# Prompt attention: which engine multiplies the probabilities by the reciprocal of their row's sum

## The chip, the cores and the metric

The kernel runs on one core of one Trainium2 chip. The metric is the device time of one execution in microseconds. The core has five instruction queues that run side by side and meet only at semaphores: TensorE (PE, with its weight loads PEld), VectorE (DVE), ScalarE (ACT), GpSimd (POOL) and SyncE (SP), which issues DMAs.

## The reference

The program is one step of a two-layer encoder: latent attention, a gated MLP mixer, and a squared-ReLU MLP behind each. The change lies in the attention of the 1024 prompt tokens, 8 heads:

```python
s = jnp.einsum('bqhd,bkhd->bhqk', qn, kn) + jnp.einsum('bqhr,bkr->bhqk', qr, kr)
s = s.astype(jnp.float32) * scale
visible = (k_pos[None, :] // CHUNK) <= (q_pos[:, None] // CHUNK)
s = jnp.where(visible[None, None], s, jnp.finfo(jnp.float32).min)
pr = jax.nn.softmax(s, axis=-1).astype(ckv.dtype)
```

The softmax is computed as exp(s - max) and then a multiplication by 1 / sum of the row. The probabilities then multiply the values.

## The kernel before

All matrix products are made in three passes: each float32 operand is held as a high part and a low part, and `mm3` multiplies hi by hi, hi by lo and lo by hi. ScalarE makes a high part by copying with rounding, VectorE makes the low part by subtracting the high part from the original.

`prompt_attention_phase` takes the heads two at a time, in four pairs. Each pair has a first stage, which projects queries, keys and values for 8 tiles of 128 tokens, and a second stage of 16 units, which is what the change touches. Unit n is 128 queries of one head: units 0 to 7 belong to the first head, 8 to 15 to the second. Because of the causal mask its width is 256, 256, 512, 512, 768, 768, 1024, 1024 keys, and the same again for the second head. Two units (2g, 2g+1) make a group of 256 queries, and the product with the values is made for a group at once.

One unit passes through these steps:

- `scores(n)`, TensorE: the scores into PSUM, in one bank up to 512 keys and two beyond. It waits for the exponentials of unit n-2, whose banks it takes.
- `maxes(n)`, VectorE: the row maximum (L949) and its negative times the scale (L950).
- `exps(n)`, ScalarE: exp of PSUM into `pr` in SBUF (L843), which also sums each row; a short second instruction of the same line reads the sum out to `total`.
- `normalise(n)`, VectorE: the reciprocal of `total` into `inv` (L955), then `pr` times `inv` in place (L956), which gives `pr_ready`.
- `probsT(n)`, TensorE: transposes of `pr` in 128 x 128 tiles into PSUM bank 4 or 5 (L1082), in one chunk of up to four tiles, or two chunks for more than 512 keys. A chunk waits until the chunk two before it has been read by both other engines (`pT_ready`).
- `probsT(n)`, ScalarE and VectorE: the high part of each chunk (L852), then its low part (L965).
- `values(g)`, TensorE: the three-pass product with the values, once both units of the group are transposed and split; ScalarE copies the result out (L859).

The order on each queue is fixed by the program, and every wait is for a semaphore's count. In turn n the queues hold:

- TensorE: scores of n+2, in turns 0, 6 and 14 one step of an unrelated modulation product (`mod1_step`, L157), transposes of n, and in even turns from 2 on the values of group n/2 - 1. Behind the last turn come the projection of the next pair's first tile (not in the last pair) and the values of group 7.
- VectorE: maximum of n+1, normalise n, low part of n-1; in turns 1, 9 and 14 small additions for the modulation, and in turns 13 and 14 the low part of the next pair's weights (L1202, not in the last pair).
- ScalarE: exponentials of n, high part of n-1, in even turns from 4 on a result copy; in turns 13 and 14 the high part of the next pair's weights (L1197, not in the last pair).

`mx`, `neg`, `total` and `inv` have two columns and `pr` two rows, used by turns for even and odd units.

Of the kernel before, what the change touches and what calls it, by code (L numbers as in the profile page):

```python
# [19 lines left out]
ALU = mybir.AluOpType  # L20
ACT = mybir.ActivationFunctionType
AX = mybir.AxisListType

P = 128
# [561 lines left out]
def prompt_attention_phase(nc, psum, io, ident, c_silu, cqT, ckvT, krT, ahead):  # L586
    PAIRS = H // 2
    QT = QL // P
    T = SEQ // P
    GR = T // 2  # L590
    N = 2 * 2 * GR
# [7 lines left out]
    def key_tiles(n):  # L599
        return 2 * unit(n)[1] + 2  # L600
# [11 lines left out]
    with Phase(nc, "patt") as ph:  # L612
# [41 lines left out]
        s_ready = ph.sem("s_ready")  # L654
        max_ready = ph.sem("max_ready")
        exp_ready = ph.sem("exp_ready")
        pr_ready = ph.sem("pr_ready")
        pT_raw = ph.sem("pT_raw")
        pT_hi_ready = ph.sem("pT_hi_ready")
        pT_ready = ph.sem("pT_ready")  # L660
# [21 lines left out]
        with nc.Block() as block:  # L682
# [111 lines left out]
            @block.scalar  # L794
            def _(act):
                def tile(p, t):
                    b, s = 2 * (t % 3), t % 2
                    act.wait_ge(proj_ready, p * T + (1 + t + 1))
                    act.wait_ge(r_ready, p * T + (t + 1))
                    act.wait_ge(ss_ready, p * T + (t + 1))  # L800
                    q, kv = psum[:, b, :], psum[:, b + 1, :]
                    HW = DN + DR
                    act.activation(v_hi[:, t, :], kv[:, 2 * DN:], ACT.Copy)
                    for n, (src, c) in enumerate((
                            (q[:, 0:DN], 0), (q[:, HW:HW + DN], HW), (q[:, DN:HW], DN), (q[:, HW + DN:2 * HW], HW + DN),
                            (kv[:, 0:DN], QW), (kv[:, DN:2 * DN], QW + DN))):
                        last = act.activation(junk[:, c:c + src.shape[1]], src, ACT.Square, accum_out=ss[:, s, n:n + 1])
                    last.then_inc(ss_ready, 1)

                def keys(p, t):  # L810
                    b, s = 2 * (t % 3), t % 2
                    act.wait_ge(r_ready, p * T + (2 + t + 1))
                    act.wait_ge(tokT_raw, p * T + (t + 1))
                    for j in range(2):
                        last = act.activation(k_tok[:, s, j, :], psum[:, b + 1, j * DN:(j + 1) * DN], ACT.Copy,
                                              scale=rs[:, s, 4 + j:5 + j])
                    last.then_inc(ktok_ready, 1)

                def tileT(p, t):
                    b, toks = 6, slice(t * P, (t + 1) * P)  # L820
                    act.wait_ge(tokT_raw, p * T + (2 + t + 1))
                    act.activation(qT_hi[:, :, toks], psum[:, b, :].rearrange("p (k n) -> p k n", k=4), ACT.Copy)
                    act.activation(kT_hi[:, :, toks], psum[:, b + 1, 0:2 * P].rearrange("p (k n) -> p k n", k=2),
                                   ACT.Copy).then_inc(tokT_hi_ready, 1)

                def guest(p):
                    q, k, HW = psum[:, 0, :], psum[:, 1, :], DN + DR
                    act.wait_ge(guest_raw, p + 1)
                    act.activation(guest_q, q[:, 0:QW], ACT.Copy)
                    for n, (src, c) in enumerate((  # L830
                            (q[:, 0:DN], 0), (q[:, HW:HW + DN], HW), (q[:, DN:HW], DN), (q[:, HW + DN:2 * HW], HW + DN),
                            (k[:, 0:DN], QW), (k[:, DN:2 * DN], QW + DN))):
                        last = act.activation(junk[:, c:c + src.shape[1]], src, ACT.Square,
                                              accum_out=ahead.ss_s[:, p, n:n + 1])
                    last.then_inc(guest_ready, 1)

                def exps(p, n):
                    s, width = n % 2, key_tiles(n) * P
                    if n == 5:
                        act.wait_ge(guest_stored, 16 * (p + 1))  # L840
                    act.wait_ge(max_ready, p * N + (n + 1))
                    act.wait_ge(pT_raw, p * C + (1 + before[max(n - 1, 0)]))
                    act.activation(pr[:, s, 0:width], flat(score_bank(n), width), ACT.Exp, bias=neg[:, s:s + 1], scale=SCALE,  # L843
                                   accum_out=total[:, s:s + 1]).then_inc(exp_ready, 1)

                def probsT(p, n):
                    g, i = n // 2, n % 2
                    for c, (k0, k1) in enumerate(chunks[n]):
                        m = before[n] + c
                        act.wait_ge(pT_raw, p * C + (1 + m + 1))  # L850
                        act.wait_ge(pv_ready, p * GN + (g + 1))
                        act.activation(pT_hi[g % 2][:, k0:k1, i * P:(i + 1) * P],  # L852
                                       psum[:, 4 + m % 2, 0:(k1 - k0) * P].rearrange("p (k n) -> p k n", n=P),
                                       ACT.Copy).then_inc(pT_hi_ready, 1)

                def out(p, g):
                    act.wait_ge(pv_ready, p * GN + (2 + g + 1))
                    act.wait_ge(stored[g % 2], p * (16 * GN // 2) + 16 * (g // 2 + 1))
                    act.activation(o[:, g % 2, :], psum[:, 6 + g % 2, 0:2 * P], ACT.Copy).then_inc(o_ready, 1)  # L859

                def w_split(p, i):
                    act.wait_ge(raw_in, p * 32)
                    act.wait_ge(proj_ready, p * T + 1)
                    ahead.split_hi(act, i)

                def pair(p, last):
                    for t in range(T + 1):
                        if t < T:
                            tile(p, t)
                        if t >= 1:  # L870
                            keys(p, t - 1)
                        if t >= 2:
                            tileT(p, t - 2)
                    guest(p)
                    exps(p, 0)
                    exps(p, 1)
                    tileT(p, T - 1)
                    for n in range(1, N + 1):
                        if 1 < n < N:
                            exps(p, n)  # L880
                        probsT(p, n - 1)
                        if n >= 4 and n % 2 == 0:
                            out(p, n // 2 - 2)
                        if n in SPLIT and not last:
                            w_split(p + 1, SPLIT.index(n))
                    out(p, GN - 1)

                act.sem_inc(ss_ready, 1)
                act.sem_inc(exp_ready, 2)
                act.sem_inc(o_ready, 2)  # L890
                for p in range(PAIRS):
                    pair(p, p == PAIRS - 1)

            @block.vector
            def _(dve):
# [53 lines left out]
                    step.run(dve.reduce_max(mx[:, s:s + 1], flat(score_bank(n), width), AX.X))  # L949
                    dve.tensor_scalar(neg[:, s:s + 1], mx[:, s:s + 1], -SCALE, None, ALU.mult).then_inc(max_ready, 1)  # L950

                def normalise(p, n, step):
                    s, width = n % 2, key_tiles(n) * P
                    dve.wait_ge(exp_ready, p * N + (2 + n + 1))
                    step.run(dve.reciprocal(inv[:, s:s + 1], total[:, s:s + 1]))  # L955
                    dve.tensor_scalar(pr[:, s, 0:width], pr[:, s, 0:width], inv[:, s:s + 1], None, ALU.mult  # L956
                                      ).then_inc(pr_ready, 1)

                def probsT(p, n):
                    g, i = n // 2, n % 2  # L960
# [7 lines left out]

                def pair(p, last):
                    step = Steps(dve, dve_step)  # L970
                    step.base = p * (2 * T + 2 * N + 6 + 4)
                    for t in range(T + 1):
                        if t >= 2:
                            tileT(p, t - 2, step)
# [3 lines left out]
                            finish_mod1(p, 0, step)  # L978
                    maxes(p, 0, step)
                    maxes(p, 1, step)  # L980
                    normalise(p, 0, step)
                    tileT(p, T - 1, step)
                    for n in range(1, N + 1):
                        if n + 1 < N:
                            maxes(p, n + 1, step)
                        if n < N:
                            normalise(p, n, step)
                        if n == 14:
                            read_mod1(p, 3)
                        probsT(p, n - 1)  # L990
                        if n in (1, 9):
                            read_mod1(p, 1 + n // 9)
                            finish_mod1(p, 1 + n // 9, step)
                        if n in SPLIT and not last:
                            ahead.split_lo(dve, p + 1, SPLIT.index(n))
                    finish_mod1(p, 3, step)
                    assert step.n == 2 * T + 2 * N + 6 + 4

                dve.sem_inc(mod_ready, 1)
                dve.sem_inc(mod1_ready, 1)  # L1000
# [10 lines left out]
            def _(pe):  # L1011
# [62 lines left out]
                    mm.then_inc(s_ready, 1)  # L1074

                def probsT(p, n):
                    pe.wait_ge(pr_ready, p * N + (n + 1))
                    for c, (k0, k1) in enumerate(chunks[n]):
                        m = before[n] + c
                        pe.wait_ge(pT_ready, p * C + (m + 1))  # L1080
# [2724 lines left out]
```

## Time and profile before

| | us |
|---|---|
| median of 3 runs | 2758.52 |
| lowest and highest | 2758.33, 2760.22 |
| the profiled execution's own time | 2763.28 |
| its span, first to last instruction | 2761.4 |

The profile gives for each group of instructions its line, engine, operation, output and inputs, shapes and count, then busy time and the mean length of one in ns. "Idle before" is the time for which the engine stood still before them, with what it waited for. In a timeline the columns are start, length, engine, line, operation and tiles, and in brackets the idle time before and its releaser. Instructions of one engine overlap a little at their ends, and a row with x2 merges neighbours. A matmul's end is modelled; its start is recorded. The second pair's 16 units lie between 280 and 339 us of the span, and the stages of the four pairs repeat each other closely.

### The profile page before, as it was taken

The page shows a single profiled execution, that of the slowest core. Times are in us where ns is not written, and L with a number is a line of the kernel's source. Part 1 is how long each engine was busy: PE and PEld are TensorE (multiplying, and loading weights), DVE is VectorE, ACT ScalarE, POOL GpSimd, SP SyncE. Part 2 cuts the span into 40 slices and gives each one's busy share as a digit, 9 for nine tenths or more (in the row PEclk, how much of TensorE's full clock was granted, in tenths as well). Part 3 has the DMA queues.
Part 4 walks back from the last instruction along what each step waited for, and adds up shares of the span by engine and source line. Part 5 has one row for each costly group of instructions (what it writes and reads, how often), then busy time and mean ns, then how long its engine had stood idle before and what let it go on. Part 6 is the DMA issues. An engine that isn't in the chain of part 4 may idle for free.

```text
span 2761.4 us, 45430 instructions
## 1 busy us (share of the span) xinstructions
PE 2649.2 (96%) x16628; PEld 2355.7 (85%) x16628; DVE 1878.2 (68%) x2672; ACT 1145.3 (41%) x2330; POOL 804.3 (29%) x736
## 2 busy tenths in 40 slices
PE   7989999899999999999999998999989999999998
PEld 4978888789997899999788887888879999988886
DVE  4677787655565876666898976224596666788886
ACT  3365556445552432222454444223342222354452
POOL 1122012055661222221144543000132222134444
PEclk9999999999999999999999999999999999999999
DMA  6244334322243333344534357124534333634446
GB/s 239 84 148 163 133 137 145 114 86 69 68 171 107 123 120 136 137 141 152 196 128 153 130 186 206 31 65 138 172 102 147 134 134 134 223 123 154 135 141 130
DMA packets 238061, 375.11 MB, mean 136 GB/s; under 512 B 18932, under 2 KB 182932, under 8 KB 234584
## 3 DMA queue, kind: packets, MB, share of 16 engines
q1 hardware_dynamic: 234408, 360.23, 39.0%
q0 software_dynamic: 3504, 12.91, 2.3%
q8 instruction: 92, 1.51, 0.2%
q14 instruction: 57, 0.47, 0.1%
HBM read 276.60 MB, written 96.48 MB: 135 GB/s over the span
## 4 chain that ended last, share of the span: by engine, by line
PE 54%; issue 6%; DVE 4%; DMA 2%; POOL 1%; ACT 1%; SPq 0%; POOLq 0%; DVEq 0%; ACTq 0%
PE psum L110 18%; PE psum L112 18%; PE psum L111 18%; DMA scratch_x_mid<-half_acc 1%; DVE half_h_lo L3052 1%; PE psum L3599 1%; DVE half_acc L3239 0%; POOL half_small L2899 0%; DMA half_m<-scratch_mixT 0%; DMA gate_x<-scratch_x_mid 0%; ACT half_tmp L2712 0%; PE psum L3610 0%; PE psum L3570 0%; DVE half_h_raw L3071 0%; SPq L134 0%
## 5 line engine op out<-in xcount | busy, mean ns | idle before, releaser
L2935 POOL TENSOR_TENSOR half_acc<-half_acc,half_tmp 128x512 f32<-128x512 f32 x174 | 292.2, 1693 | 356.0 <-ACT half_tmp L2712 268.8
L2712 ACT ACTIVATE half_tmp<-psum 128x512 f32<-128x512 f32 x174 | 104.0, 598 | 300.8 <-PE psum L112 300.6
L3239 DVE TENSOR_TENSOR half_acc<-half_acc,psum 128x512 f32<-128x512 f32 x240 | 160.5, 679 | 72.1 <-PE psum L112 53.3
L2605 ACT ACTIVATE half_snap_u<-psum 128x288 f32<-128x288 f32 x128 | 52.6, 411 | 285.8 <-PE psum L112 285.8
L110 PE MATMUL psum<-half_h_hi,half_w0q_hi 128*128 128x288 f32 x512 | 152.2, 297 | 7.2 <-DVE half_h_lo L3052 6.0
L110 PE MATMUL psum<-half_h_hi,half_w1q_hi 128*128 128x288 f32 x512 | 151.7, 296 | 1.6 <-DVE half_w1q_lo L3078 1.6
L111 PE MATMUL psum<-half_h_lo,half_w1q_hi 128*128 128x288 f32 x512 | 151.0, 295 | 0.0
L111 PE MATMUL psum<-half_h_lo,half_w0q_hi 128*128 128x288 f32 x512 | 151.0, 295 | 0.0
L112 PE MATMUL psum<-half_h_hi,half_w1q_lo 128*128 128x288 f32 x512 | 150.6, 294 | 0.0
L112 PE MATMUL psum<-half_h_hi,half_w0q_lo 128*128 128x288 f32 x512 | 150.5, 294 | 0.0
L3097 DVE TENSOR_TENSOR half_piece<-psum,half_snap_u 128x576 f32<-128x576 f32 (+1 forms) x68 | 49.1, 722 | 106.4 <-PE psum L112 79.0
L110 PE MATMUL psum<-half_w_hi,half_m_hi 128*128 128x512 f32 x288 | 117.0, 406 | 3.4 <-DVE half_w_lo L3010 1.8
L110 PE MATMUL psum<-half_h_hi,half_w0r_hi 128*128 128x288 f32 x384 | 115.1, 300 | 5.0 <-DVE half_h_lo L3052 5.0
L110 PE MATMUL psum<-gate_w_hi,gate_hT_hi 128*128 128x512 f32 x288 | 114.9, 399 | 2.0 <-issue 1.2
L112 PE MATMUL psum<-half_w_hi,half_m_lo 128*128 128x512 f32 x288 | 114.3, 397 | 0.0
L111 PE MATMUL psum<-half_w_lo,half_m_hi 128*128 128x512 f32 x288 | 114.1, 396 | 0.0
L111 PE MATMUL psum<-half_h_lo,half_w0r_hi 128*128 128x288 f32 x384 | 113.9, 297 | 0.0
L110 PE MATMUL psum<-half_h_hi,half_w1r_hi 128*128 128x288 f32 x384 | 113.7, 296 | 0.0
L112 PE MATMUL psum<-half_h_hi,half_w0r_lo 128*128 128x288 f32 x384 | 113.5, 296 | 0.0
L111 PE MATMUL psum<-half_h_lo,half_w1r_hi 128*128 128x288 f32 x384 | 113.3, 295 | 0.0
L112 PE MATMUL psum<-half_h_hi,half_w1r_lo 128*128 128x288 f32 x384 | 112.9, 294 | 0.0
L112 PE MATMUL psum<-gate_w_hi,gate_hT_lo 128*128 128x512 f32 x288 | 112.7, 391 | 0.0
(742 smaller groups left out, 8950.6 us busy)
## 6 DMA issues: line engine op xcount, KB each, us to landing
scratch_hid<-half_piece SPq DMA_DIRECT2D x64, 576.0 KB, 4.2
patt_mod_w<-in_ada_w_ffn SPq DMA_DIRECT2D x32, 768.0 KB
half_w0q_raw<-in_w SPq DMA_DIRECT2D x24, 1024.0 KB, 5.0
half_w1q_raw<-in_w SPq DMA_DIRECT2D x24, 1024.0 KB, 5.0
scratch_hid_sums<-half_sum SPq DMA_DIRECT2D x96, 256.0 KB, 2.8
patt_mod_w<-in_ada_w_att SPq DMA_DIRECT2D x16, 1024.0 KB, 5.0
half_s0q_raw<-scratch_hid SPq DMA_DIRECT2D x22, 512.0 KB
half_s1q_raw<-scratch_hid SPq DMA_DIRECT2D x22, 512.0 KB, 4.0
```

The lines of the kernel that those rows point to most:

```text
L110: pe.matmul(out, a_hi, b_hi, start=first, stop=False, skip_group_check=go_on)
L111: pe.matmul(out, a_hi, b_lo, start=False, stop=False, skip_group_check=go_on)
L112: return pe.matmul(out, a_lo, b_hi, start=False, stop=last, skip_group_check=go_on)
L2605: act.activation(out[:, grp, :], psum[:, bank(product, grp), 0:GN], ACT.Copy).then_inc(a.c.snap, 1)
L2712: act.activation(out, psum[:, o_bank_of(product, j), :], ACT.Copy).then_inc(a.c.taken, 1)
L2935: pool.tensor_tensor(part, part, snapshot(a, n, m), ALU.add).then_inc(a.c.added, 1 if i % SLABS else 3)
L3052: dve.tensor_tensor(a.h_lo[grp][slot][:], a.h_raw[grp][slot][:], f(a.h_hi[grp][slot][:]), ALU.subtract).then_inc(a.lo_ready[grp], 1)
L3097: dve.tensor_tensor(a.piece[i.par][f_][:, cols, side, :], psum[:, b:b + len(grps), 0:GN], snap[:, cols, :], ALU.add).then_inc(a.c.hid_read, 1)
L3239: dve.tensor_tensor(part, part, of, ALU.add).then_inc(a.c.read, 1)
L3599: mm = pe.matmul(psum[:, 6 + i // 4, (i % 4) * P:(i % 4 + 1) * P], g.ws[:, int(t == SAMPLE), i, :], g.z[:, t % 2, D + i * P:D + (i + 1) * ...
```

## The change

The multiplication by the reciprocal moves from VectorE to ScalarE, as a Copy activation whose scale is the column `inv`, in place on `pr`. VectorE keeps the reciprocal alone (`invert`), gives a new semaphore `inv_ready`, and ScalarE waits for it. `pr_ready` is given by ScalarE and starts two higher; VectorE now waits before a reciprocal until the multiplication two units before has read that column of `inv`. On ScalarE the new instruction stands behind the exponentials of the same unit and ahead of the high part of the unit before. The order on VectorE and TensorE stays.

```diff
@@ scalar queue
+                def normalise(p, n):
+                    s, width = n % 2, key_tiles(n) * P
+                    act.wait_ge(inv_ready, p * N + (n + 1))
+                    act.activation(pr[:, s, 0:width], pr[:, s, 0:width], ACT.Copy, scale=inv[:, s:s + 1]
+                                   ).then_inc(pr_ready, 1)
+
@@
                     guest(p)
                     exps(p, 0)
                     exps(p, 1)
+                    normalise(p, 0)
                     tileT(p, T - 1)
                     for n in range(1, N + 1):
                         if 1 < n < N:
                             exps(p, n)
+                        if n < N:
+                            normalise(p, n)
                         probsT(p, n - 1)
@@
+                act.sem_inc(pr_ready, 2)
@@ vector queue
-                def normalise(p, n, step):
-                    s, width = n % 2, key_tiles(n) * P
+                def invert(p, n):
+                    s = n % 2
                     dve.wait_ge(exp_ready, p * N + (2 + n + 1))
-                    step.run(dve.reciprocal(inv[:, s:s + 1], total[:, s:s + 1]))
-                    dve.tensor_scalar(pr[:, s, 0:width], pr[:, s, 0:width], inv[:, s:s + 1], None, ALU.mult
-                                      ).then_inc(pr_ready, 1)
+                    dve.wait_ge(pr_ready, p * N + (2 + n - 1))
+                    dve.reciprocal(inv[:, s:s + 1], total[:, s:s + 1]).then_inc(inv_ready, 1)
@@
                         if n + 1 < N:
                             maxes(p, n + 1, step)
                         if n < N:
-                            normalise(p, n, step)
+                            invert(p, n)
@@ tensor queue
                 def probsT(p, n):
-                    pe.wait_ge(pr_ready, p * N + (n + 1))
+                    pe.wait_ge(pr_ready, p * N + (2 + n + 1))
```

## Rows read from the trace of the kernel before

**Rows 1.** The page's first part: busy time, share of the span, instructions.
```profile
PE 2649.2 (96%) x16628; PEld 2355.7 (85%) x16628; DVE 1878.2 (68%) x2672; ACT 1145.3 (41%) x2330; POOL 804.3 (29%) x736
```

**Rows 2.** Busy time by stretch: the second pair's units; then VectorE on `pr` alone.
```profile
core 0: us, PE busy (x) PEld busy (x) DVE busy (x) ACT busy (x) POOL busy (x), PEclk, DMA share, GB/s
280.00:339.00 59.00, 57.44 (x571) 49.33 (x564) 43.73 (x105) 30.11 (x68) 1.14 (x2) 1.00 0.36 126
...
280.00:339.00 59.00, 8.86 (x16) 1.00 0.36 126
```

**Rows 3.** What TensorE waited for, 184 to 532 us: total, times, longest.
```profile
PE psum L1082 <- DVE patt_pT_lo L965: 5.3, 8, 1.1
PE psum L110 <- DVE patt_pT_lo L965: 1.6, 1, 1.6
```

**Rows 4.** ScalarE by line and shape, 184 to 532 us: busy, mean ns.
```profile
L852 ACT ACTIVATE patt_pT_hi<-psum 128x512 fp32r<-128x512 f32 x64 | 36.6, 597 | 62.8 <-PE psum L1082 62.8
L843 ACT ACTIVATE patt_pr<-psum,patt_neg 128x1024 f32<-128x1024 f32 x16 | 18.0, 1125 | 0.7
L843 ACT ACTIVATE patt_pr<-psum,patt_neg 128x768 f32<-128x768 f32 x16 | 14.5, 905 | 1.1
L843 ACT ACTIVATION_READ_ACCUMULATOR patt_pr<-psum,patt_neg 128x1 f32 x64 | 12.8, 200 | 0.0
L859 ACT ACTIVATE patt_o<-psum 128x256 f32<-128x256 f32 x32 | 12.3, 385 | 18.4 <-PE psum L112 18.4
L843 ACT ACTIVATE patt_pr<-psum,patt_neg 128x512 f32<-128x512 f32 x16 | 11.0, 690 | 7.5 <-DVE patt_neg L950 7.4
L843 ACT ACTIVATE patt_pr<-psum,patt_neg 128x256 f32<-128x256 f32 x16 | 7.7, 480 | 0.9 <-DVE patt_neg L950 0.9
```

**Rows 5.** ScalarE by line and shape, the whole program.
```profile
L1197 ACT ACTIVATE patt_wq_hi<-patt_q_raw 128x1152 fp32r<-128x1152 f32 x4 | 4.7, 1176 | 0.0
L1197 ACT ACTIVATE patt_wkv_hi<-patt_kv_raw 128x1024 fp32r<-128x1024 f32 x4 | 4.3, 1075 | 0.0
L1574 ACT ACTIVATE satt_o<-psum,satt_inv 128x256 f32<-128x256 f32 x8 | 3.8, 475 | 16.2 <-PE psum L1827 16.2
L843 ACT ACT_TABLE_LOAD x1 | 1.3, 1283 | 0.0
```

**Rows 6.** VectorE by line and shape, 184 to 532 us.
```profile
L965 DVE TENSOR_TENSOR patt_pT_lo<-psum,patt_pT_hi 128x512 fp32r<-128x512 f32 x64 | 42.4, 683 | 4.8 <-ACT patt_pT_hi L852 4.8
L949 DVE TENSOR_REDUCE patt_mx<-psum 128x1 f32<-128x1024 f32 x16 | 19.6, 1225 | 10.9 <-PE psum L1073 10.9
```

**Rows 7.** Timeline of three engines in turn 6 of the second pair (TensorE, ScalarE, VectorE rows).
```profile
299.25 0.82 PE L1082 MATMUL psum<-ident,patt_pr 128*128 128x128 f32 x6
...
299.45 1.23 DVE L949 TENSOR_REDUCE patt_mx<-psum 128x1 f32<-128x1024 f32 x1 [1.44 <-PE psum L1073]
...
300.78 0.15 DVE L955 RECIPROCAL patt_inv<-patt_total 128x1 f32<-128x1 f32 x1
...
299.89 0.87 ACT L852 ACTIVATE patt_pT_hi<-psum 128x512 fp32r<-128x512 f32 x2 [2.29 <-PE psum L1082]
...
302.47 1.06 PE L1082 MATMUL psum<-ident,patt_pr 128*128 128x128 f32 x8 [0.23 <-DVE patt_pT_lo L965]
```

**Rows 8.** Timeline of turns 13 to 15 of the second pair (VectorE, then TensorE rows).
```profile
324.24 1.35 DVE L1202 TENSOR_TENSOR patt_wq_lo<-patt_q_raw,patt_wq_hi 128x1152 fp32r<-128x1152 f32 x1
325.76 1.23 DVE L949 TENSOR_REDUCE patt_mx<-psum 128x1 f32<-128x1024 f32 x1 [0.17 <-PE psum L1073]
...
327.10 0.15 DVE L955 RECIPROCAL patt_inv<-patt_total 128x1 f32<-128x1 f32 x1
327.28 0.75 DVE L956 TENSOR_SCALAR patt_pr<-patt_pr,patt_inv 128x1024 f32<-128x1024 f32 x1
...
328.12 1.01 DVE L965 TENSOR_TENSOR patt_pT_lo<-psum,patt_pT_hi 128x512 fp32r<-128x512 f32 x2
...
328.94 1.06 PE L1082 MATMUL psum<-ident,patt_pr 128*128 128x128 f32 x8 [1.10 <-DVE patt_pT_lo L965]
331.99 0.38 PE L1082 MATMUL psum<-ident,patt_pr 128*128 128x128 f32 x2
```

**Rows 9.** Busy time by stretch around one fall of the clock, in a later stage.
```profile
1665.00:1667.50 2.50, 0.47 (x2) 0.42 (x3) 2.50 (x4) 2.15 (x4) 0.67 (x1) 1.00 0.46 187
1667.50:1670.90 3.40, 3.40 (x10) 2.65 (x9) 0.53 (x1) 1.79 (x4) 2.40 (x5) 0.50 0.85 122
```

More of the change, by code:

```diff
@@ L656, in prompt_attention_phase @@
         exp_ready = ph.sem("exp_ready")
-        pr_ready = ph.sem("pr_ready")
+        inv_ready, pr_ready = ph.sem("inv_ready"), ph.sem("pr_ready")
         pT_raw = ph.sem("pT_raw")
@@ L970, in pair @@
                     step = Steps(dve, dve_step)
-                    step.base = p * (2 * T + 2 * N + 6 + 4)
+                    step.base = p * (2 * T + N + 6 + 4)
                     for t in range(T + 1):
@@ L980, in pair @@
                     maxes(p, 1, step)
-                    normalise(p, 0, step)
+                    invert(p, 0)
                     tileT(p, T - 1, step)
@@ L996, in pair @@
                     finish_mod1(p, 3, step)
-                    assert step.n == 2 * T + 2 * N + 6 + 4
+                    assert step.n == 2 * T + N + 6 + 4
                 dve.sem_inc(mod_ready, 1)
```

## The prediction

> **What bounds the kernel now.** I read the page's busy times first: TensorE is busy for 96% of the span, ScalarE for 41% [rows 1]. An average says little about one stage, so I took the second pair's 16 units alone: of 59.0 us TensorE is busy for 57.4, VectorE for 43.7, ScalarE for 30.1 [rows 2]. The stage is TensorE's, and a microsecond counts only where TensorE stands still for it. Third, its waits: over all four pairs its matmuls wait 5.3 us in 8 places for the low part of the transposed probabilities before a transpose, and 1.6 us once before a value product [rows 3]. The multiplication itself is not what they wait for: in turn 14 it ends at 328.03, and the transposes start at 328.94, behind the first half of L965 [rows 8]. ScalarE has room by the average, but what matters is where: it stands idle for 62.8 us before the high parts of 512 columns, for TensorE's transposes [rows 4]. The change puts its instruction exactly ahead of those. Two timelines of the second pair show how near the chain runs to TensorE there [rows 7, 8].
>
> **What goes from VectorE.** Sixteen multiplications per pair, 8.86 us [rows 2], 35 us in all. VectorE is not the bound, so this is worth only what it shortens of TensorE's waits.
>
> **What comes to ScalarE.** Sixteen Copy activations per pair, SBUF to SBUF, with a per-partition scale. No row of before is exactly that. The exponentials have the same widths, the same float32 and one per-partition operand: 0.48, 0.69, 0.905 and 1.125 us for 256, 512, 768 and 1024 [rows 4]. A copy from SBUF without such an operand takes 1.075 for 1024 [rows 5], one from PSUM 0.385 for 256 and 0.597 for 512 [rows 4]. A copy of 256 with a per-partition scale takes 0.475 [rows 5], as long as the exponential of 256, so I take the exponentials' lengths: 4 x (0.48 + 0.69 + 0.905 + 1.125) = 12.8 us per pair, 51 in all. The lower bound is the plain copies' (0.385, 0.60, 0.84 by interpolation, 1.075), and, far from it, the length that VectorE needed. The upper bound is an exponential with its readout of 0.20 [rows 4].
>
> The 0.475 beside 0.385 says that a per-partition operand costs 0.09 us. The Trainium skill ("ScalarE: Activation LUTs", What ACT_TABLE_LOAD costs) states the same, about 93 ns for each such operand and 280 ns + 0.833 ns per column with one; by it 1024 columns would take an estimated 1.133 us, and the sum below would change by under 1 us. It speaks for the exponentials' row over the plain copies'.
>
> **What moves: the order.** The new waits matter more than the lengths. The multiplication of n waits for `inv` of n. On VectorE that reciprocal stands behind the maximum of n+1, which waits for the scores of n+1 on TensorE. Queued behind the waiting instruction on ScalarE are the high part of n-1 and the exponentials of n+1. For the high part wait the low part, the transposes that need its bank and the value product; for the exponentials waits the product of scores two units on. Before, the high part ran while VectorE still made the maximum: in turn 6 it starts at 299.89, the reciprocal comes only at 300.78 [rows 7]. Now it starts behind reciprocal and multiplication. VectorE's new wait, for the multiplication two units back, costs nothing: ScalarE ran it one turn earlier, ahead of the exponentials whose sum the same reciprocal needs.
>
> **The sum.** I laid the rows' lengths end to end in program order for one pair, each instruction starting when its engine is free and its semaphores have come. Neighbours overlap by 0.08 to 0.1, a hop between engines takes 0.03 to 0.05, and 0.12 from the low part to TensorE. Laid so for the kernel before, the last value product of the second pair starts at 335.6, the trace has 335.8, and the waits come where the trace has them (0.46 and 1.36 against 0.23 and 1.10 in the two places below). With the change:
>
> - Transposes of unit 6. The scores of 7 are there at 299.4. Then maximum, negation, reciprocal 1.23 + 0.15 + 0.15 with gaps of 0.1, 1.6; multiplication 1.125; high part 0.60; low part 0.68; hops 0.2 less overlap 0.1: 4.1. TensorE has work of its own for about 2.6 (from 299.25 to 302.47, less what it waited and the end of the scores) [rows 7]. It waits 1.45 in place of 0.46: +1.0.
> - Transposes of unit 14. From the reciprocal's end on, before: 0.75, 0.25 less overlap, and the first half of the low part, 1.66 to 328.94 [rows 8]. Now 1.125 + 0.60 + 0.68 with hops, 2.50: +0.84. The maximum of 15 also starts later. Before, VectorE had split the weights (1.35) by 325.6, just ahead of the scores at 325.7 [rows 8]. Now ScalarE's half of the split (1.18 [rows 5]) stands behind the multiplication of 13 (0.905) and the high part of 12, so VectorE's half ends 1.05 behind the scores. Together +1.9, a wait of 3.2 in place of 1.36.
> - Transposes of unit 15. From the start of 14's transposes: 0.40 + 0.60 for them and the first high part, then on ScalarE 0.385, 0.385, the second weight split 1.075, exponentials 1.125 + 0.20, reciprocal 0.15, multiplication 1.125, high part 0.60, low part 0.68, less overlaps: 4.6. TensorE has 2.9 to 3.05 of work until then [rows 8]. +1.6, where it hardly waited.
> - Twelve small places where the same chain comes 0.1 to 0.6 too late: scores of 4 by 0.41 (the exponentials of 2 now follow a multiplication and a high part), transposes of 8 by 0.58, value product 0 by 0.35, the second chunks of 4 and 12 by 0.29 each, and seven of 0.10 to 0.22. Together +3.1.
>
> That is 1.0 + 1.9 + 1.6 + 3.1 = 7.6 us per pair. The last pair has no weight splits: unit 14 costs 0.8, unit 15 0.65, the others as before, and its final value product waits 0.2 less: 5.5. Sum: 3 x 7.6 + 5.5 = 28.3. Nothing behind the stage hides it: the next pair's first ScalarE work waits for the last value product, and the next phase starts at a barrier. The profiled time goes from 2763.3 to 2791.6; it lies 4.8 above the median, so the median goes from 2758.5 to 2786.8, about 2787.
>
> With the multiplication at zero length the same layout gives only +1.3, with VectorE's lengths (0.355 to 0.755) +17.0, with the plain copies' +24.4, with the readout on top +39. So the length of the new instruction inside the chain is nearly all of it.
>
> **The rivals.**
>
> Shorter instruction: ScalarE runs it as fast as VectorE did. +17.0, 2775.5. Against it stands every SBUF row of ScalarE [rows 5].
>
> Hidden after all: the idle time of ScalarE before the high parts (62.8 us [rows 4], 2.29 of it in turn 6 [rows 7]) takes the multiplication in, and VectorE's relief comes off TensorE's waits: 0.75 in each of the four places at unit 14, 0.23 at each unit 6, 0.75 at the last value product [rows 3, 7, 8]. That is -4.7, 2753.8, not slower. It decides by whether the reciprocal is ready before the transposes of n-1 are. In turn 6 it is 0.9 late [rows 7].
>
> The clock: TensorE works at its upper level (1.00, 2.4 GHz) all through the stage. In a later stage it did 0.47 us of work in 2.5 us, and the clock then stood at 0.50 (1.2 GHz) for 3.4 us [rows 9]. A 3.2 us wait at unit 14 is longer than any before in these stages. A fall of 3.4 us costs 1.7 us of work, but it would fall on the value product ahead of unit 15's 1.6 us wait, which takes it in. A longer fall would cost up to 1.7 us in each pair: +28 to +35; with a somewhat longer instruction up to +39, 2797.5.
>
> Table loads: if Copy with a scale and Exp needed different tables, 128 loads of 1.28 us [rows 5] would come in, +164. One load serves the stage now, copies included, so this is remote.
>
> **How the numbers follow.** Forecast 2787 (+28, within +24 to +32): 0.60. Longer or with the clock, up to 2798: 0.20. Shorter, about 2775.5: 0.12. Hidden: 0.07, of which 0.02 for a gain over 0.2%. Table loads 0.01. The range 2775.5 to 2798 takes in both bounds of the length and the clock. A measurement can tell about 0.2%, 5.5 us, from no change: faster 0.02, within 0.06, slower 0.92.
>
> **What would show it.** ScalarE should have 64 new rows in place of L956 with means near 0.48, 0.69, 0.905 and 1.125. VectorE's idle time before L965 should grow from 4.8 us [rows 6] to some 80 us, since it now waits for the high part each turn. TensorE should stand still before the transposes of unit 14 for about 3.2 us in three pairs and 2.2 in the last, and for 1.6 before unit 15. The first stage of each pair should be as long as before. The prediction is wrong at its core if the high part still starts right behind the transposes, if the new means lie under 0.4 of a microsecond for 256, or if the pairs' unit stages grow by less than 4 us each.

## The result and the profile after

| | before | after |
|---|---|---|
| median of 3 runs, us | 2758.52 | 2786.66 |
| lowest and highest | 2758.33, 2760.22 | 2785.05, 2790.81 |
| the profiled execution's own time | 2763.28 | 2790.81 |
| its span | 2761.4 | 2789.1 |

The ratio is 1.0104, with a 95% interval of 1.009 to 1.0119. That is +28.1 us, between +25 and +33: slower, and by about what was forecast (+28.3).

First the new instruction. ScalarE by line and shape in the kernel after, 184 to 562 us (count, busy us, mean ns, idle time before with its releaser):

```profile
L858 ACT ACTIVATE patt_pT_hi<-psum 128x512 fp32r<-128x512 f32 x64 | 35.8, 582 | 4.3 <-PE psum L1091 4.3
L849 ACT ACTIVATE patt_pr<-patt_pr,patt_inv 128x1024 f32<-128x1024 f32 x16 | 18.4, 1150 | 15.7 <-DVE patt_inv L966 15.7
L849 ACT ACTIVATE patt_pr<-patt_pr,patt_inv 128x768 f32<-128x768 f32 x16 | 15.0, 937 | 16.2 <-DVE patt_inv L966 16.2
L849 ACT ACTIVATE patt_pr<-patt_pr,patt_inv 128x512 f32<-128x512 f32 x16 | 11.6, 724 | 25.3 <-DVE patt_inv L966 25.3
...
L849 ACT ACTIVATE patt_pr<-patt_pr,patt_inv 128x256 f32<-128x256 f32 x16 | 8.1, 508 | 20.9 <-DVE patt_inv L966 20.9
```

The multiplications (L849) take 0.508, 0.724, 0.937 and 1.150 us for 256 to 1024 columns, 53.1 us in all, which is some 0.03 each more than the exponentials of the same widths [rows 4]. The idle time has moved. Before, ScalarE stood 62.8 us ahead of the high parts of 512 columns, waiting for transposes [rows 4], and 84.9 us with those of 256. In the kernel before, all widths, 184 to 532 us:

```profile
ACT patt_pT_hi L852 <- PE psum L1082: 84.9, 60, 3.1
```

Now it stands 4.3 us there, and 78.1 us (all widths) ahead of the multiplications, waiting for the reciprocal.

What waited for what, all engines and then TensorE alone, 184 to 562 us (total, times, longest):

```profile
DVE patt_pT_lo L974 <- ACT patt_pT_hi L858: 82.7, 64, 1.7
ACT patt_pr L849 <- DVE patt_inv L966: 78.1, 60, 3.2
...
PE psum L1091 <- DVE patt_pT_lo L974: 17.8, 14, 3.1
PE psum L157 <- DMA patt_mod_tab<-in_ada_tab_ffn: 1.6, 3, 0.8
PE psum L110 <- DVE patt_pT_lo L974: 1.5, 1, 1.5
PE psum L1091 <- ACT patt_pr L849: 1.1, 4, 0.6
```

VectorE waits for the high part in each of the 64 units, 82.7 us where it was 4.8 [rows 6]. TensorE's transposes wait 17.8 us for the low part where it was 5.3 [rows 3], and now in 4 places for the multiplication itself, 1.1 us.

TensorE's longest wait in each pair is the one before the transposes of unit 14. Here it is in the first pair: turns 13 to 15 of the kernel after, VectorE's, ScalarE's and TensorE's rows of the timeline.

```profile
232.84 1.36 DVE L1211 TENSOR_TENSOR patt_wq_lo<-patt_q_raw,patt_wq_hi 128x1152 fp32r<-128x1152 f32 x1 [0.31 <-ACT patt_wq_hi L1206]
234.12 1.22 DVE L959 TENSOR_REDUCE patt_mx<-psum 128x1 f32<-128x1024 f32 x1
...
235.45 0.16 DVE L966 RECIPROCAL patt_inv<-patt_total 128x1 f32<-128x1 f32 x1
...
237.31 1.02 DVE L974 TENSOR_TENSOR patt_pT_lo<-psum,patt_pT_hi 128x512 fp32r<-128x512 f32 x2 [1.50 <-ACT patt_pT_hi L858]
...
235.65 1.15 ACT L849 ACTIVATE patt_pr<-patt_pr,patt_inv 128x1024 f32<-128x1024 f32 x1 [1.74 <-DVE patt_inv L966]
236.70 0.85 ACT L858 ACTIVATE patt_pT_hi<-psum 128x512 fp32r<-128x512 f32 x2
...
237.71 1.07 ACT L1206 ACTIVATE patt_wkv_hi<-patt_kv_raw 128x1024 fp32r<-128x1024 f32 x1
238.65 1.13 ACT L843 ACTIVATE patt_pr<-psum,patt_neg 128x1024 f32<-128x1024 f32 x1
...
240.14 1.15 ACT L849 ACTIVATE patt_pr<-patt_pr,patt_inv 128x1024 f32<-128x1024 f32 x1 [0.27 <-DVE patt_inv L966]
...
238.15 1.07 PE L1091 MATMUL psum<-ident,patt_pr 128*128 128x128 f32 x8 [3.05 <-DVE patt_pT_lo L974]
242.65 1.16 PE L1091 MATMUL psum<-ident,patt_pr 128*128 128x128 f32 x8 [1.30 <-DVE patt_pT_lo L974]
```

Read by start time, this is the chain of the prediction: reciprocal 235.45, multiplication 235.65, high part 236.70, low part 237.31, transposes 238.15, with TensorE idle for 3.05 us. From the start of the reciprocal to that of the transposes 2.70 us pass; before it was 1.84 [rows 8].

How long each pair takes. The last row of each pair on ScalarE is the copy of the last group's result. Before, then after:

```profile
241.83 0.39 ACT L859 ACTIVATE patt_o<-psum 128x256 f32<-128x256 f32 x1 [4.88 <-PE psum L112]
338.87 0.39 ACT L859 ACTIVATE patt_o<-psum 128x256 f32<-128x256 f32 x1 [4.88 <-PE psum L112]
435.63 0.39 ACT L859 ACTIVATE patt_o<-psum 128x256 f32<-128x256 f32 x1 [4.87 <-PE psum L112]
531.31 0.38 ACT L859 ACTIVATE patt_o<-psum 128x256 f32<-128x256 f32 x1 [3.75 <-PE psum L112]
```

```profile
249.64 0.39 ACT L865 ACTIVATE patt_o<-psum 128x256 f32<-128x256 f32 x1 [4.92 <-PE psum L112]
354.36 0.39 ACT L865 ACTIVATE patt_o<-psum 128x256 f32<-128x256 f32 x1 [4.92 <-PE psum L112]
459.30 0.39 ACT L865 ACTIVATE patt_o<-psum 128x256 f32<-128x256 f32 x1 [4.92 <-PE psum L112]
562.04 0.38 ACT L865 ACTIVATE patt_o<-psum 128x256 f32<-128x256 f32 x1 [5.24 <-PE psum L112]
```

The pairs are longer by 8.1 (7.8, and 0.3 for an earlier start of the stage), 7.7, 8.2 and 7.1 us. That is 31.0 for all four pairs, called the stage below, reckoned from its first exponential to the next phase's first transposes: 352.3 before, 383.3 after. What follows took 2225.1 us before and 2222.1 after, and the start was 0.3 shorter. So the profiled total of +27.7 is +31.0 and -3.3. The first stages are untouched: from a pair's last result copy to ScalarE's copy of 384 columns just ahead of the next pair's exponentials (L829), 36.2 us pass in both kernels.

### The profile page after: what moved, and what is told of

Read it like the earlier page. It is cut to its first block, busy times and chain, and to the rows that moved or that the text cites. A ratio compares the mean times of both kernels' runs of the same rounds, so it can differ in the third digit from the quotient of the medians.

```text
span 2789.1 us, 45493 instructions
## 1 busy us (share of the span) xinstructions
PE 2654.4 (95%) x16628; PEld 2355.8 (84%) x16628; DVE 1848.4 (66%) x2608; ACT 1188.0 (43%) x2394; POOL 800.8 (29%) x736
## 4 chain that ended last, share of the span: by engine, by line
PE 53%; issue 6%; DVE 5%; DMA 2%; POOL 1%; ACT 1%; SPq 0%; POOLq 0%; DVEq 0%; ACTq 0%
PE psum L110 18%; PE psum L112 17%; PE psum L111 17%; DMA scratch_x_mid<-half_acc 1%; DVE half_h_lo L3061 1%; PE psum L3608 1%; DVE half_acc L3248 0%; DMA half_m<-scratch_mixT 0%; POOL half_small L2908 0%; DMA gate_x<-scratch_x_mid 0%; ACT half_tmp L2721 0%; PE psum L3619 0%; PE psum L3579 0%; DVE half_h_raw L3080 0%; SPq L134 0%
## 5 line engine op out<-in xcount | busy, mean ns | idle before, releaser
L111 PE MATMUL psum<-gate_w_lo,gate_hT_hi 128*128 128x512 f32 x288 | 112.6, 391 | 0.0
```

The costliest lines, as they stand in the source:

```text
L111: pe.matmul(out, a_hi, b_lo, start=False, stop=False, skip_group_check=go_on)
```

## The experiments

The theory: the loss comes from one chain. Reciprocal behind the next unit's maximum, multiplication, then high part and low part, since the multiplication stands ahead of the high part. The rivals are that ScalarE's 53 us of added work cost time wherever they stand; that the clock's falls are a large part; and that the weight splits near a pair's end are a cause of their own. All lengths of the stage below are of the profiled execution, reckoned as above; ratios are against the kernel before on the same chip.

| run | change to the kernel after (e6: to the kernel before) | laid out beforehand | stage, against 352.3 | ratio, 95% interval |
|---|---|---|---|---|
| the change itself | | +28.3 | +31.0 | 1.0104 (1.009 to 1.0119) |
| e1 | reciprocal first | -0.4 | +1.4 | 0.9992 (0.9982 to 1.0001) |
| e2 | multiplication behind the high part | +3.5 | +7.4 | 1.0005 (0.9994 to 1.0015) |
| e3 | a second pass on ScalarE | +71 | +74.8 | 1.0254 (1.0236 to 1.0271) |
| e4 | no wait for the reciprocal | -3.0 | -0.5 | 0.9991 (0.9982 to 1.0001) |
| e5 | half the columns | +16.4 | +18.1 | 1.0055 (1.0037 to 1.0073) |
| e9 | splits in turns 9 and 10 | +31 | +32.3 | one execution, 2788.7 us, beside a median of 2760.4 |
| e7 | e1 and e9 together | -3.5 | -0.3 | 0.9985 (0.9975 to 0.9994) |
| e6 | the kernel before, reciprocal first | -1.9 | -0.4 | 1.0004 (0.9992 to 1.0016) |

The column in the middle is the same laying out of lengths as in the prediction, with the measured lengths of L849 from e1 on.

### The reciprocal first

```diff
 vector queue
-                        if n + 1 < N:
-                            maxes(p, n + 1, step)
                         if n < N:
                             invert(p, n)
+                        if n + 1 < N:
+                            maxes(p, n + 1, step)
```

> The changed kernel, with VectorE's reciprocal of unit n ahead of the maximum of unit n+1, in place of behind it. Nothing else differs; ScalarE does the same 64 multiplications. Chain theory (the multiplication, standing ahead of the high part of n-1, waits for a reciprocal that waits for the next unit's scores): the loss goes nearly all, laid out from the rows -0.4 us against the kernel before, so 2753 to 2763. ScalarE's idle time before the multiplications falls from 73 us to under 25. Rival 1 (ScalarE's added work, 51 us, is what costs, wherever it stands): still +20 to +30, about 2785. Rival 2 (a large part is the falls of the clock in this stage, one in each of four places of the changed kernel): they go only with the long waits, so this run can't tell it from the chain theory alone.

ScalarE's multiplications are as many and as long as in the change, but what they wait for has shrunk. The waits of all engines, and TensorE's (184 to 610 us, here and in the runs below, which takes in the whole stage):

```profile
ACT patt_pr L849 <- DVE patt_inv L966: 29.0, 60, 2.3
DVE patt_pT_lo L974 <- ACT patt_pT_hi L858: 18.9, 24, 1.7
ACT patt_pT_hi L858 <- PE psum L1091: 18.7, 17, 1.8
...
PE psum L1091 <- DVE patt_pT_lo L974: 6.5, 7, 1.1
```

29.0 in place of 78.1, 18.9 in place of 82.7, and 6.5 in place of 17.8. ScalarE's wait was expected under 25 and is 29.0. The time is that of the kernel before. The same 53 us of ScalarE's work cost nothing that can be measured, so the work as such is not the cause.

### The multiplication behind the high part

```diff
 scalar queue
-                        if n < N:
-                            normalise(p, n)
                         probsT(p, n - 1)
+                        if n < N:
+                            normalise(p, n)
```

> The changed kernel, with ScalarE's multiplication of unit n behind the high part of unit n-1, in place of ahead of it. VectorE's order as in the change. Chain theory: the high part starts again right behind the transposes, and only the transposes of n wait for the multiplication, which has the time of the scores of n+2 as cover; laid out +3.5 us against the kernel before, so 2759 to 2766. VectorE's idle time before the low parts falls from 83 us to under 15. Rival 1 (ScalarE's work as such): +20 to +30. If both this run and the one with the reciprocal first come near the kernel before, the loss needs both orders at once.

```profile
ACT patt_pT_hi L858 <- PE psum L1091: 42.3, 35, 3.5
ACT patt_pr L849 <- DVE patt_inv L966: 14.8, 45, 0.9
DVE patt_pT_lo L974 <- ACT patt_pT_hi L858: 12.0, 18, 1.6
...
PE psum L1091 <- ACT patt_pr L849: 7.0, 8, 1.1
```

The high part waits for the transposes again (42.3 us), and VectorE for the high part only 12.0. TensorE now waits for the multiplication itself, 7.0 us in 8 places. The ratio is within 0.2% of one. Either of the two orders, mended alone, takes the loss away, as far as the medians can tell. The profiled execution was the slowest of the ten, and its stage is 3.9 longer than laid out. Most of that rest can be the clock, which was at its lower level twice in this stage, each time at the first units of a pair, where the layout has it at the upper one (length, then PE, PEld, DVE, ACT and POOL busy, granted clock, DMA share, GB/s):

```profile
282.70:286.10 3.40, 3.40 (x16) 2.13 (x18) 1.44 (x5) 1.56 (x5) 0.00 (x0) 0.51 0.00 0
480.70:484.10 3.40, 3.40 (x23) 2.13 (x24) 1.64 (x6) 1.43 (x5) 3.40 (x1) 0.50 0.02 5
```

Work at half the clock for 3.4 us costs at most 1.7, so 3.4 of the 3.9 at most; what it did cost was not measured by itself.

### No wait for the reciprocal

ScalarE multiplies by a column of ones. The division by the row's sum is left out.

```diff
 scalar queue
-                    act.wait_ge(inv_ready, p * N + (n + 1))
-                    act.activation(pr[:, s, 0:width], pr[:, s, 0:width], ACT.Copy, scale=inv[:, s:s + 1]
+                    act.wait_ge(exp_ready, p * N + (2 + n + 1))
+                    act.activation(pr[:, s, 0:width], pr[:, s, 0:width], ACT.Copy, scale=unit_scale[:]
```

> The changed kernel, where ScalarE's multiplication takes a column of ones, so it doesn't wait for the reciprocal but only for its own exponentials; VectorE makes the reciprocals as before, and nobody reads them. It leaves out the division by the row's sum. ScalarE's work has the same length and place as in the change. Chain theory: without the wait the loss is gone, laid out -3.0 us against the kernel before, 2752 to 2759. Rival 1 (ScalarE's work as such, or its place ahead of the high part): +15 to +28.

```profile
L851 ACT ACTIVATE patt_pr<-patt_pr,patt_unit_scale 128x1024 f32<-128x1024 f32 x16 | 18.4, 1152 | 0.5
...
PE psum L1094 <- DVE patt_pT_lo L977: 4.3, 4, 1.1
```

The instruction is as long (1.152 us) and in the same place, ahead of the high part, and the loss is gone. Ahead of the high part the instruction does no harm so long as it doesn't wait for the reciprocal.

### Longer and shorter

A second pass, which copies `pr` onto itself, and half the columns. The half leaves out the division of each row's other half.

```diff
 scalar queue, second pass
-                                   ).then_inc(pr_ready, 1)
+                                   ).then_inc(act_step, 1)
+                    act.wait_ge(act_step, p * N + (n + 1))
+                    act.activation(pr[:, s, 0:width], pr[:, s, 0:width], ACT.Copy).then_inc(pr_ready, 1)
 scalar queue, half the columns
-                    act.activation(pr[:, s, 0:width], pr[:, s, 0:width], ACT.Copy, scale=inv[:, s:s + 1]
+                    act.activation(pr[:, s, 0:width // 2], pr[:, s, 0:width // 2], ACT.Copy, scale=inv[:, s:s + 1]
```

> The changed kernel, and ScalarE copies each unit's multiplied probabilities once more onto themselves (64 more Copy activations without a per-partition operand, 0.385 to 1.06 us, 46 us in all) before it gives them free. Chain theory, laid out: +71 us against the kernel before, 2830, that is 43 more than the change for 46 us of added work, since the chain is now late at every unit. Rival 1 (ScalarE's work is a load with much room): the same 0.55 us per us of added work as in the change, +53, 2812. Hidden elsewhere: under +40.

> The changed kernel, with ScalarE multiplying only the first half of each row's columns (128, 256, 384 or 512 in place of 256 to 1024), 0.39 to 0.72 us each, 35 us in all in place of 52. It leaves out the division of the other half. Chain theory, laid out: +16.4 us against the kernel before, stage and total alike, 2775 to 2779; the wait before unit 14's transposes 2.5 us in place of 3.1. Rival (the loss is in the order and the hops, the length hardly counts): +25 or more. Rival (clock falls make up much of the loss): it would drop sharply where waits get under 2 us, and here they stay above, so +20.

With the second pass (16.9 us for its 16 of 1024, 47 us in all), TensorE's waits are:

```profile
L853 ACT ACTIVATE patt_pr<-patt_pr 128x1024 f32<-128x1024 f32 x16 | 16.9, 1057 | 0.5
...
PE psum L1094 <- DVE patt_pT_lo L977: 36.3, 29, 4.6
PE psum L1094 <- ACT patt_pr L853: 8.3, 11, 1.4
PE psum L110 <- ACT patt_pr L844: 7.1, 13, 0.6
```

The places in which the transposes wait for the low part go from 14 to 29, and the stage grows by 43.8 us for 47 us of added work: nearly one for one. With half the columns:

```profile
L849 ACT ACTIVATE patt_pr<-patt_pr,patt_inv 128x512 f32<-128x512 f32 x16 | 11.6, 723 | 17.3 <-DVE patt_inv L966 17.3
...
PE psum L1091 <- DVE patt_pT_lo L974: 14.4, 15, 2.3
```

17 us less work (0.400, 0.510, 0.616 and 0.723 us each) take 12.9 off the stage. So each microsecond on the chain costs 0.75 near the change's length and 0.93 beyond it, while the change's 53 us cost 31. These prices hold some of the clock: 1.5 of the 12.9 is a fall in the change's last pair (see below), without which it is 0.67, and with the second pass the clock stood at its lower level for 37 us of the stage, where it was 14 with the change. The layout, which has no falls, gives 43 for the second pass all the same. It is a chain with slack that runs out unit by unit, not a load of one price.

### The weight splits earlier

```diff
-    SPLIT = (13, 14)
+    SPLIT = (9, 10)
```

> The changed kernel, with the two weight splits in turns 9 and 10 in place of 13 and 14. Chain theory, laid out: the wait before unit 14's transposes falls from 3.1 to 2.2 us and that before unit 15's from 1.3 to 0.7, as in the last pair, but new waits of 0.6 to 1.0 come up at the scores of 13 and 14 and the transposes of 11, so the stage is as long as with the change, +31 against the kernel before. If the splits' place at the end were a cause of its own, the stage would be 5 us shorter.

TensorE's rows with a wait in the second pair, from turn 11 on:

```profile
327.34 0.50 PE L110 MATMUL psum<-patt_kT_hi,patt_qT_hi 128*128 128x512 f32 x1 [0.45 <-ACT patt_pr L843]
329.83 0.66 PE L1091 MATMUL psum<-ident,patt_pr 128*128 128x128 f32 x4 [0.35 <-ACT patt_pr L849]
331.20 0.50 PE L110 MATMUL psum<-patt_kT_hi,patt_qT_hi 128*128 128x512 f32 x1 [0.71 <-ACT patt_pr L843]
342.75 1.06 PE L1091 MATMUL psum<-ident,patt_pr 128*128 128x128 f32 x8 [1.97 <-DVE patt_pT_lo L974]
```

The wait before unit 14 is 1.97 in place of 3.06, and three waits come up in turns 11 and 12, of 0.35 to 0.71 (0.6 to 1.0 were expected). The stage is as long as with the change, in the one execution that there is. With this order of the queues, the splits decide where the chain is late, not how much.

### The order on VectorE in the kernel before, and a version that is faster

```diff
 the kernel before, vector queue
-                        if n + 1 < N:
-                            maxes(p, n + 1, step)
                         if n < N:
                             normalise(p, n, step)
+                        if n + 1 < N:
+                            maxes(p, n + 1, step)
```

> The kernel before, VectorE multiplying, but with reciprocal and multiplication of unit n ahead of the maximum of n+1. Laid out -1.9 us against the kernel before, 0.1%, within what a measurement tells from no change. If it gained 5 us or more, the order on VectorE would be worth something by itself and the gain of the run with the reciprocal first wouldn't speak for the chain alone.

> The changed kernel with the reciprocal of n ahead of the maximum of n+1, and with the weight splits in turns 9 and 10 in place of 13 and 14: a try at a version that is faster than both. Laid out -3.5 us against the kernel before, of it 3 from the wait before unit 15's transposes, which goes. The stage was 1.4 longer than before with the reciprocal first alone, where the layout gave -0.4, so -1.5 is as likely. TensorE has at most some 10 us of waits in this stage to win.

The order by itself gives the kernel before nothing: 1.0004, stage -0.4. The kernel after with the reciprocal first and the splits in turns 9 and 10 is faster than the kernel before, by 0.15% (0.9985, 0.9975 to 0.9994). That is small, and its profiled stage is only 0.3 shorter, where 3.5 was laid out, so the profile doesn't show where the gain lies.

## Why the prediction was right

**The length of the instruction.** Forecast 0.48, 0.69, 0.905, 1.125; measured 0.508, 0.724, 0.937, 1.150. The exponentials' row was the right one, 0.03 short. The Trainium skill ("ScalarE: Activation LUTs", What ACT_TABLE_LOAD costs) gives 280 ns + 0.833 ns per column with a per-partition operand; by it 1024 columns would take an estimated 1.133 us, 0.017 below the 1.150 measured. It also gives about 93 ns for each such operand, and the trace agrees: in the run with the second pass, 1024 columns take 1.149 us with the operand and 1.057 without.

**The order.** The step that mattered. ScalarE waited 78 us for reciprocals and VectorE 83 us for high parts (forecast "some 80"). The runs e1, e2 and e4 each cut the chain at another link, and in each the median came back to within 0.1% of the kernel before (the interval of e2 reaches up to +4 us).

**Unit 14.** Forecast a wait of 3.2 in three pairs and 2.2 in the last; measured 3.05, 3.06, 3.08 and 1.97, in place of 1.10. The step from the reciprocal on was forecast at +0.84 and is +0.86.

**Unit 15.** Forecast 1.6 and 0.65; measured 1.30 in the first pair and 0.32 in the last. From 14's transposes to 15's, 4.6 us was forecast and 4.50 measured, but the items listed for it don't add up to that: they come to 6.7, or 5.7 at the least with the overlaps taken off. The trace shows why. ScalarE's second weight split starts at 237.71, ahead of 14's transposes at 238.15, so the list's first four items (the transposes, a first high part, two of 0.385) are no links of this chain. It is the split, exponentials, reciprocal, multiplication, high part and low part alone, less the 0.44 by which the split starts earlier.

**Unit 6.** Forecast 1.45 in place of 0.46; in the first pair the trace has 0.42, and 0.75 just ahead of it in the same turn. TensorE's rows of turn 6:

```profile
206.28 1.53 PE L157 MATMUL psum<-patt_mod_w,c_silu 128*32 128x96 f32 x64 [0.75 <-DMA patt_mod_tab<-in_ada_tab_ffn]
208.23 1.06 PE L1091 MATMUL psum<-ident,patt_pr 128*128 128x128 f32 x8 [0.42 <-DVE patt_pT_lo L974]
```

The 0.75 I had not seen coming: the modulation step waits for its table, whose load SyncE issues behind the store of group 0's result. The transposes behind it have to wait for the same chain anyway: the two waits are 0.75 and 0.42, 0.37 and 0.81, 0.47 and 0.70 in the first three pairs, so the first shifts and their sum stays at 1.17 or 1.18. That is +0.94 on the 0.23 of before, against +1.0, but SyncE's queue should have been named.

**The small places.** Forecast +3.1 in each pair. In the first pair the trace names three: 0.55 before the transposes of unit 1, 0.55 before the scores of 4 (forecast 0.41) and 0.47 before the transposes of 8 (forecast 0.58). What is left of that pair's 8.1 is 2.3 us, which stands in no row of a wait. TensorE's busy time in the pair grew by as much, from 57.52 to 59.81 us, with the same 571 products and a clock of 1.00 in both kernels. The ends of matmuls are modelled, so this can be waits too short to show; that is not shown.

**The sum.** Three pairs at 8.1, 7.7 and 8.2 against 7.6, and the last at 7.1 against 5.5 (its own terms, 1.0 + 0.8 + 0.65 + 3.1 - 0.2, add up to 5.35). The multiplications are 1.9 us longer in all than forecast, 53.1 against 51.2, and at 0.67 to 0.75 for each that makes 28.3 into an estimated 29.6 or 29.7. The rest of the stage's 31.0 is about the size of the clock's fall in the last pair.

**The clock.** It was a rival and it came, and its price was about as bounded. Before, the clock had not fallen between the first exponential and the last value product (granted clock 1.00 from 180 to 531 us). After, it fell four times there, for 3.4 us each: in the second pair, twice in the third, and in the fourth. Busy time by stretch in the kernel after (length, then PE, PEld, DVE, ACT and POOL busy, granted clock, DMA share, GB/s):

```profile
338.00:342.60 4.60, 1.81 (x68) 1.43 (x66) 3.06 (x6) 2.86 (x7) 0.00 (x0) 0.98 0.01 4
342.60:346.00 3.40, 3.13 (x16) 3.16 (x17) 1.76 (x4) 3.13 (x5) 0.57 (x1) 0.53 0.67 158
...
557.60:561.00 3.40, 3.40 (x17) 3.40 (x17) 0.16 (x1) 0.00 (x0) 0.00 (x0) 0.52 0.14 43
```

In the second pair TensorE did 1.81 us of work in 4.6, and then ran at its lower level, 1.2 GHz (granted clock 0.50), for 3.4 us. The transposes of unit 15 follow those of unit 14 by 4.49 us there (342.87 to 347.36), and by 4.50 in the first pair, where the clock held: the 1.3 us wait took the fall in, as argued, and likewise in the third (447.79 to 452.39, 4.60). The third pair's other fall, at 393.6, was not foreseen: it follows a wait of 1.83 that stands in the kernel before too, with no fall behind it. Three short waits that the second pair has at the same units, 0.98 us together, are gone with it, and the pair is 0.5 us longer than the second. In the last pair the fall lies on the final value product, with nothing behind it to hide in. From its start to the copy of its result 4.68 us pass (557.36 to 562.04), and 3.14 before (528.17 to 531.31): 1.5 us.

**Where luck helped.** The stage took 31.0 us more, 2.7 above the forecast, and what follows it took 3.0 less. That part of the kernel is the same code. Over ten profiled kernels it took 2217.8 to 2226.2 us, and the clock stood at its lower level for 46 to 82 us of an execution, in 6 to 14 stretches. That the median hit the forecast to 0.2 us (+28.1 against +28.3) is in part chance; the mechanism's own number is 31.0 against 28.3.

**The other rivals.** No further table load came in. The multiplication was not as short as VectorE's. It was hidden only where its order was mended.

## What to carry to other kernels

An engine that is idle half the time can still be the wrong place for a step. Ask what stands behind the new instruction on its queue, and what the new wait itself waits for. Here two facts met that are harmless apart: the reciprocal stood behind the next unit's maximum, and the multiplication stood ahead of the high part. Either alone cost under 0.2%, both together 1.0%. When work moves to another engine, put the producer of its operand first in its own queue; that was one swap of two lines.

## What the runs showed of the hardware

- Waits of 3.05, 3.06 and 3.08 us at the same place of three pairs were followed by a fall of TensorE's clock to 1.2 GHz in the last two and by none in the first, and falls also came behind waits of 1.8 us. A fall of 3.4 us cost 0 and 0.1 us where a wait came behind it, and 1.5 us where none did.
- A Copy from SBUF to SBUF with a per-partition scale takes 0.092 us more than one without, for 1024 columns (1.149 and 1.057, the run with the second pass), and 0.03 more than an exponential of the same width from PSUM (1.150 and 1.122, the change).
- ScalarE needs 1.150 us where VectorE needed 0.753 for the same multiplication of 1024 float32 columns.
